# Recurrent part of a hybrid decoder layer: chunks of one 128-token tile instead of 64 tokens, groups of heads written out

## The chip, the core and the metric

The kernel runs on one core of one Trainium2 chip. The metric is the time of one execution on the device in microseconds, the median over several runs. The core has five engines that work side by side and meet at semaphores: PE (TensorE, matrix products, writes only to PSUM), DVE (VectorE), ACT (ScalarE), POOL (GpSimd) and SP, which here only issues DMAs. Each engine takes its instructions strictly in the order written.

## The reference, cut to what matters

One layer on x (256 tokens, 2048 wide), in float32: half a SwiGLU step, an input projection into an attention group and a recurrent group (RWKV-7), an output projection over both, half a SwiGLU step again, and a gated embedding. The change touches only the recurrent group, 16 heads of 64:

```
def step(state, inp):
    r_t, w_t, k_t, v_t, kk_t, a_t = inp
    sa = einsum('bhvk,bhk->bhv', state, -kk_t)
    state = (state * w_t[:, :, None, :]
             + sa[..., None] * (kk_t * a_t)[:, :, None, :]
             + v_t[..., None] * k_t[:, :, None, :])
    return state, einsum('bhvk,bhk->bhv', state, r_t)
...
decay = exp(-exp(w));  kk = kk / max(norm(kk), 1e-12);  k = k * (1 + (a - 1) * k_a)
o = (o - mean(o)) * rsqrt(var(o) + GN_EPS) * ln_x_w + ln_x_b
o = (o + sum(r * k * r_k) * v) * g
```

The recurrence over tokens isn't run token by token. Within a chunk of tokens it is a triangular system, which is inverted; from chunk to chunk a state of 64 x 64 per head is carried.

## The kernel before, in words

The order of the whole kernel is written out by hand, one program for each engine. Feed-forward, projections and the rest are products of three parts (`products`, L339 to L341) on weights that ACT and DVE split into a high and a low half (`split_hi` L316, `split_lo` L325). Between the input projection and the output projection lie attention (`pe_mla` and its counterparts) and then the recurrent part. It takes four heads at a time, a group, four groups in all (`GROUPS`). The 256 tokens are two tiles (`TT`) of 128. Each group has eight systems (`systems`): two tiles, two pairs of heads, two heads of a pair.

A group passes through these steps.

Loads and front. SP loads a group's r, k, v and the same rows one token earlier, with the parameters (`rwkv_loads`), once the group before has handed over v (`v_handed`) and made its inputs (`front_ready`). POOL mixes the two (`shift`, L915 and L923), and takes a square root (`power`, L662) for the unit keys. PE makes the gates in three parts (`pe_gates`, L1024 to L1037), with ACT behind each (`act_gates`), the last two giving cumulated decays within a chunk of 64 tokens. DVE does `front` in steps 1 to 5 (unit keys, mixed keys, the bonus) and `with_decay`, which multiplies four inputs by the decays.

Scores. PE turns the four inputs (`turn`, L1050), ACT and DVE copy them out (`act_alpha`, `act_scores`, `scores`), and PE multiplies all tokens of a tile with all (`pe_scores`, L1061 and L1067), 256 columns a product; DVE masks the result to the part of the triangle that lies within a chunk (L1353, tiles `AB` and `AK`).

Inverse. `pe_inverse` (L1079, L1089), `act_inverse` (L1237) and DVE's `inverse` (L1379, L1366) double the size of the inverted blocks level by level. `INV` has five levels, 2, 4, 8, 16, 32. A level is done in two halves `h` of four systems: PE makes q, ACT copies it to `Q`, PE makes x, DVE joins it to `XT` by a predicated copy and flips it to `X` by a transpose. The next level's q of a half waits for that half's join. Levels 0 and 1 (`EARLY`) of group r + 1 stand at the end of loop iteration r, levels 2 to 4 (`LATER`) at the start of the next. Between the `LATER` halves DVE does `front` of the following group, and PE its gates.

State. `pe_state`, `act_state` and DVE's `state` multiply the inverse by keys and values (L1105, L1110, L1115) and then go chunk by chunk, four chunks of 64 tokens: PE multiplies by the state (L1123, L1128), DVE makes U (L1405), PE adds the new state (L1135, L1136 and L1140, the last two on 64 rows), DVE scales it by a chunk's decay (L1411), ready in the tile `PCM` which POOL fills (`chunk_decay`, L930). ACT copies each chunk's output (L1267), and `add_inner` adds what comes from within the chunk (L1145, L1096).

Output. DVE centres the output by head (`out_centre`), POOL finishes it (`finish`: a scale, a power, the gate, the bonus, L915, L662 and L948), PE turns it (`pe_out`, L1163), ACT and DVE split it into the output projection's operands (`act_out`, `out_lo`). `pe_out` stands at the end of a loop iteration, so in PE's order between the `EARLY` levels of the next group and its `LATER` ones. ACT copies gate and bonus to their second tiles (`act_hand_over`) when `finish` has released them. POOL does `shift` of the next group after `finish` of the one before.

The groups run in a loop on each engine, with group 0's head and the last group's tail written out around it. After the last group PE goes on with the output projection (`w_out_block`).

## Time and profile before

| what | us |
|---|---|
| median of three runs (2259.79 to 2265.68) | 2260.6 |
| profiled execution | 2262.39 |
| its span | 2260.5 |
| PE busy in the span | 2147.1 (95%) |
| DVE busy | 1199.1 (53%) |
| ACT busy | 862.5 (38%) |
| POOL busy | 134.1 (6%) |
| groups of heads in the recurrent part | 4 |

The span is what the profile covers, from its first to its last instruction; the execution's time has the start and the end around it. Products of float32 data are two instructions each in the records (x16 stands for eight products), as are their weight loads. In a timeline row the columns are start, duration, engine, line, operation, result and inputs with their shapes, the count, and in brackets how long the engine had been idle and who released it. Rows of several instructions are merged, so their duration is from the first's start to the last's end, and the last one's end overlaps the start of what follows. The clock is PE's granted clock as a share of full speed.

### The profile page before, as it was taken

What the parts mean: (1) busy time and instruction counts of PE and PEld (TensorE: products, weight loads), DVE (VectorE), ACT (ScalarE), POOL (GpSimd) and SP (SyncE); (2) the same over time, 40 slices, a digit from 0 to 9 for tenths busy, and PEclk for the clock granted to TensorE, in tenths of its full rate; (3) what the DMA queues carried; (4) which work ended last, traced back from release to release, by engine and by line L of the source; (5) the groups of instructions that cost most, each with busy time, mean ns of one, the idle gap of its engine ahead of it and who ended that gap; (6) DMA issues with size and microseconds to landing.
All of it is one profiled execution on the core that took longest, in us unless ns stands there. A gap on an engine that the chain in (4) does not pass through costs nothing.

```text
span 2260.5 us, 25634 instructions
## 1 busy us (share of the span) xinstructions
PE 2147.1 (95%) x10216; PEld 1801.8 (80%) x10216; DVE 1199.1 (53%) x1062; ACT 862.5 (38%) x758; POOL 134.1 (6%) x83
## 2 busy tenths in 40 slices
PE   6999999999999999966988899999999999999998
PEld 5888888888887788755877788888888888888777
DVE  4455554555555544755656644555445555554644
ACT  5333333333333444523222233533333333333353
POOL 0000000000000000130334310000000000000000
PEclk9999999999999999987989999999999999999999
DMA  6555555555555476520111135555555555555444
GB/s 225 188 193 196 186 186 196 193 186 186 199 190 186 142 217 210 191 93 21 38 45 51 55 122 172 199 187 187 189 193 193 186 190 188 197 186 187 166 155 144
DMA packets 193519, 373.64 MB, mean 165 GB/s; under 512 B 6978, under 2 KB 22592, under 8 KB 193088
## 3 DMA queue, kind: packets, MB, share of 16 engines
q1 hardware_dynamic: 191888, 367.63, 49.0%
q0 software_dynamic: 1584, 5.35, 0.7%
q8 instruction: 33, 0.54, 0.1%
q14 instruction: 14, 0.11, 0.0%
HBM read 367.44 MB, written 5.52 MB: 165 GB/s over the span
## 4 chain that ended last, share of the span: by engine, by line
PE 54%; issue 36%; DVE 6%; POOL 2%; ACT 1%; DMA 1%; SPq 0%; POOLq 0%; DVEq 0%; ACTq 0%
PE PS L339 16%; PE PS L340 16%; PE PS L341 16%; DVE wlo L325 1%; POOL pv L915 1%; PE PS L1061 0%; PE PS L1089 0%; POOL zz L923 0%; PE PS L1136 0%; PE PS L389 0%; DVE sc L850 0%; PE PS L1145 0%; DMA x_resid<-in_x 0%; PE PS L354 0%; PE PS L1105 0%
## 5 line engine op out<-in xcount | busy, mean ns | idle before, releaser
L325 DVE TENSOR_TENSOR wlo<-raw,whi 128x2048 fp32r<-128x2048 f32 (+1 forms) x339 | 769.3, 2270 | 783.2 <-PE PS L341 774.3
L316 ACT ACTIVATE whi<-raw 128x2048 fp32r<-128x2048 f32 (+1 forms) x339 | 644.2, 1902 | 1035.4 <-PE PS L341 1023.6
L339 PE MATMUL PS<-whi,xT_hi 128*128 128x512 f32 (+2 forms) x1952 | 758.1, 388 | 11.0 <-DVE wlo L325 10.9
L341 PE MATMUL PS<-whi,xT_lo 128*128 128x512 f32 (+2 forms) x1952 | 754.7, 387 | 0.0
L340 PE MATMUL PS<-wlo,xT_hi 128*128 128x512 f32 (+2 forms) x1952 | 754.7, 387 | 0.0
L339 PEld LDWEIGHTS PS<-whi,xT_hi 128*128 128x128 f32 x1952 | 367.3, 188 | 86.4 <-DVE wlo L325 7.4
L341 PEld LDWEIGHTS PS<-whi,xT_lo 128*128 128x128 f32 x1952 | 367.1, 188 | 74.1
L340 PEld LDWEIGHTS PS<-wlo,xT_hi 128*128 128x128 f32 x1952 | 367.3, 188 | 72.6
L339 PE MATMUL PS<-whi,hT_hi 128*128 128x512 f32 x744 | 292.0, 392 | 6.9 <-DVE hT_lo L473 4.7
L340 PE MATMUL PS<-wlo,hT_hi 128*128 128x512 f32 x744 | 291.6, 392 | 0.0
L341 PE MATMUL PS<-whi,hT_lo 128*128 128x512 f32 x744 | 291.1, 391 | 0.0
L339 PEld LDWEIGHTS PS<-whi,hT_hi 128*128 128x128 f32 x744 | 140.8, 189 | 37.1 <-DVE hT_lo L473 5.2
L341 PEld LDWEIGHTS PS<-whi,hT_lo 128*128 128x128 f32 x744 | 141.0, 189 | 29.5
L340 PEld LDWEIGHTS PS<-wlo,hT_hi 128*128 128x128 f32 x744 | 140.8, 189 | 29.2
L482 DVE SCALAR_TENSOR_TENSOR x_resid<-PS,x_resid 128x512 f32<-128x512 f32 x184 | 118.1, 683 | 53.4 <-PE PS L341 53.4
L662 POOL TENSOR_TENSOR rstd<-rstd,con 128x2 f32<-128x2 f32 x6 | 6.2, 1042 | 1640.5 <-DVE rstd L657 1640.5
L1079 PE MATMUL PS<-XT,AB 128*128 128x128 f32 x320 | 47.4, 303 | 7.3 <-DVE XT L1379 7.0
L1079 PEld LDWEIGHTS PS<-XT,AB 128*128 128x128 f32 x320 | 43.1, 212 | 11.3 <-DVE XT L1379 8.7
L372 DVE SCALAR_TENSOR_TENSOR xT_lo<-PS,gains,xT_hi 128x256 fp32r<-128x256 f32 x64 | 26.6, 477 | 33.0 <-ACT xT_hi L363 32.9
L1237 ACT ACTIVATE Q<-PS 128x256 f32<-128x256 f32 x40 | 15.6, 389 | 72.9 <-PE PS L1079 72.9
L363 ACT ACTIVATE xT_hi<-PS,gains 128x256 fp32r<-128x256 f32 x64 | 25.2, 474 | 37.0 <-PE PS L354 37.0
L473 DVE TENSOR_TENSOR hT_lo<-PS,hT_hi 128x1024 fp32r<-128x1024 f32 x22 | 26.9, 1225 | 10.2 <-ACT hT_hi L435 10.0
(266 smaller groups left out, 1196.5 us busy)
## 6 DMA issues: line engine op xcount, KB each, us to landing
raw<-in_w_gate SPq DMA_DIRECT2D x88, 1024.0 KB, 5.0
raw<-in_w_up SPq DMA_DIRECT2D x88, 1024.0 KB, 5.0
raw<-in_w_down SPq DMA_DIRECT2D x88, 1024.0 KB, 5.0
raw<-in_w_in SPq DMA_DIRECT2D x28, 1024.0 KB, 5.4
raw<-in_w_out SPq DMA_DIRECT2D x16, 1024.0 KB, 5.0
raw<-in_w_ple_gate SPq DMA_DIRECT2D x16, 1024.0 KB, 5.1
z_scratch<-zst POOLq DMA_DIRECT2D x6, 512.0 KB, 6.2
raw<-in_w_q_b SPq DMA_DIRECT2D x3, 1024.0 KB, 5.2
```

What stands on the lines that cost most here:

```text
L316: nc.scalar.activation(whi[:, n % WHI, 0:wd], raw[:, n % RAW, 0:wd], ACT.Copy).then_inc(hi_ready, 1)
L325: nc.vector.tensor_tensor(wlo[:, n % WLO, 0:wd], raw[:, n % RAW, 0:wd], f32(whi[:, n % WHI, 0:wd]), ALU.subtract).then_inc(lo_ready, 1)
L339: nc.tensor.matmul(acc, a, whi[:, n % WHI, c], start=st, stop=False)
L340: nc.tensor.matmul(acc, a, wlo[:, n % WLO, c], start=False, stop=False)
L341: ins = nc.tensor.matmul(acc, b, whi[:, n % WHI, c], start=False, stop=en)
L363: ins = nc.scalar.activation(xT_hi[:, kt, :], PS[:, 2 + u % 2, j * SEQ:(j + 1) * SEQ], ACT.Copy, scale=gains[:, 16 * k + kt:16 * k + kt + 1])
L372: ins = nc.vector.scalar_tensor_tensor(xT_lo[:, kt, :], PS[:, 2 + u % 2, j * SEQ:(j + 1) * SEQ], gains[:, 16 * k + kt:16 * k + kt + 1], f3 ...
L473: nc.vector.tensor_tensor(hT_lo[:, :, :].rearrange("p (b j) s -> p b (j s)", b=2), PS[:, 6:8, :], f32(hT_hi[:, :, :]).rearrange("p (b j) s ...
L482: ins = nc.vector.scalar_tensor_tensor(x[:, t, j * COLS:(j + 1) * COLS], PS[:, b + t, :], factor, x[:, t, j * COLS:(j + 1) * COLS], ALU.mu ...
L915: g.tensor_tensor(o, a, b, op).then_inc(pool_chain, 1)
L1079: ins = nc.tensor.matmul(PS[:, HALF_BANKS[h][0], (s % 4) * P:(s % 4 + 1) * P], AB[:, s, 0:P], XT[:, s, :], start=True, stop=True)
L1237: nc.scalar.activation(even_cols(Q[:, 4 * h:4 * h + 4, :], l), even_cols(PS[:, HALF_BANKS[h][0], :].rearrange("p (s c) -> p s c", s=4), l) ...
```

## The change

The chunk becomes a whole tile of 128 tokens, so there are two chunks and only one update of the state, between the tiles. The decays are cumulated from the middle of a tile instead of from the start of a chunk (`cum_in`, `cum_ex`), and the state between the tiles is scaled by `between_tiles`, the product of two decays. `chunk_decay`, its tiles and the constant `two_heads` are gone. The masks cover a whole triangle. A score product becomes two, one for the first 64 tokens of a tile and one for the last 64, each 128 columns wide, the first on 64 columns of weights. The inverse gets a sixth level that joins the two halves of a tile, with products 64 columns wide. Products with values or U are 64 columns wide, one head each, where they were 128 (a pair) before. Y and the part of the output that comes from keys and values within a tile are made between the levels (`pe_value_parts`). The output is accumulated in one PSUM bank and copied once. The groups are written out instead of looped; every level and every fill has a place of its own: gates of the next group in levels 2 to 4, `out_centre` of the group before in three parts behind the half levels 1 to 3, `pe_out` and `out_lo` in level 3, `front` from the half level 5 on. POOL does `shift` of the next group first, then `finish` of the old one, `unit_keys` of the next, and `gate_norm`, which is `finish`'s first part put apart. `alpha`, `B_`, `gg` and `bonus` have two buffers, and the hand-over copies are gone.

```
-CHUNK = 64
+HC = P // 2
-        "cum_in": rate * (same & (s <= t)),
+        "cum_in": rate * ((s <= t) * 1.0 - (s < HC) * 1.0),
...
-        INV = LEVELS[1:]
-        EARLY, LATER = (0, 1), (2, 3, 4)
+        INV = LEVELS[1:] + (HC,)
+        GATES_AT = (2, 3, 4)
...
+        def score(s, bank, lhs, pr, t, par):
+            dst = PS[:, bank, (s % 2) * 256:(s % 2 + 1) * 256].rearrange("p (k c) -> p k c", k=2)
+            nc.tensor.matmul(dst[0:HC, :, 0:HC], lhs[:, par, pr, t * P:t * P + HC], ART[:, pr, t, :, 0:HC], start=True, stop=True)
+            return nc.tensor.matmul(dst[:, :, HC:P], lhs[:, par, pr, t * P:(t + 1) * P], ART[:, pr, t, :, HC:P], start=True, stop=True)
...
+        def pe_value_parts(pe, r, part):
+            if part == 0:
+                pe.wait_ge(ak_ready, 4 * r + 4)
+                pe.wait_ge(v_handed, r + 1)
+                for s, t, pr, par in systems():
+                    ins = nc.tensor.matmul(PS[:, 2, s * RN:(s + 1) * RN], AK[:, s, 0:P], vv[:, t, head(pr, par)],
+                                           start=s == 0, stop=s == 7)
+                ins.then_inc(y_done, 1)
+            elif part == 1:
+                for s, t, pr, par in systems():
+                    nc.tensor.matmul(PS[:, 3, s * RN:(s + 1) * RN], AK[:, s, P:256], vv[:, t, head(pr, par)], start=s == 0, stop=False)
+            else:
+                pe.wait_ge(heads_out, 2 + r)
+                for pr in range(2):
+                    cc = slice(pr * P, (pr + 1) * P)
+                    nc.tensor.matmul(PS[:, 2, cc], Kd[:, 0, cc], vv[:, 0, cc], start=pr == 0, stop=False)
...
 pe_inverse, behind the q products of a level:
+                if n in (1, 2, 4):
+                    pe_value_parts(pe, r, (1, 2, 4).index(n))
+                if n == 3 and r:
+                    pe_out(pe, r - 1)
+                if nxt is not None and n in GATES_AT:
+                    pe_gates(pe, nxt, n - GATES_AT[0])
...
 pe_state:
+            pe.wait_ge(up_ready, UP * r + UP)
+            pe.wait_ge(y_ready, r + 1)
+            for t in range(TT):
+                for s, _, pr, par in systems(4 * t, 4 * t + 4):
+                    ins = nc.tensor.matmul(PS[:, 6 + t, (s % 4) * RN:(s % 4 + 1) * RN], X[:, s, :], Y[:, s, :], start=s % 4 == 0, stop=s == 3)
+                ins.then_inc(w2_done, 1)
+                if t == 0:
+                    for s, _, pr, par in systems(4, 8):
+                        ins = nc.tensor.matmul(PS[:, 4, (s % 4) * P:(s % 4 + 1) * P], alpha[:, r % 2, 1, pr * P:(pr + 1) * P], X[:, s, :],
+                                               start=True, stop=True)
+                    ins.then_inc(w1_done, 1)
+            pe.wait_ge(u_ready, 2 * r + 1)
+            for pr in range(2):
+                cc = slice(pr * P, (pr + 1) * P)
+                ins = nc.tensor.matmul(PS[:, 2, cc], B_[:, r % 2, 0, cc], U[:, 0, cc], start=False, stop=pr == 1)
+            ins.then_inc(ds_done, 1)
+            own_tokens(pe, 0)
+            if nxt is not None:
+                turn(pe, nxt, 0)
+            pe.wait_ge(w1_ready, r + 1)
+            pe.wait_ge(s_ready, 2 * r + 2)
+            for pr in range(2):
+                ins = nc.tensor.matmul(PS[:, 7, pr * P:(pr + 1) * P], W1T[:, pr, :], S[:, pr, :], start=False, stop=pr == 1)
+            ins.then_inc(ws_done, 1)
+            for pr in range(2):
+                nc.tensor.matmul(PS[:, 3, 256 + pr * P:256 + (pr + 1) * P], ART[:, pr, 1, 1, :], S[:, pr, :], start=False, stop=False)
+            if nxt is not None:
+                turn(pe, nxt, 1)
+                turn(pe, nxt, 2)
+            pe.wait_ge(u_ready, 2 * r + 2)
+            own_tokens(pe, 1).then_inc(ou_done, 1)
+            if nxt is not None:
+                turn(pe, nxt, 3)
...
 DVE inverse, behind the join and flip of a half level:
+                        fill = 2 * n + h
+                        if r and fill in (1, 2, 3):
+                            out_centre(r - 1, fill - 1)
+                        if r and n == 3 and h == 1:
+                            out_lo(r - 1)
+                        if nxt is not None and fill >= 5:
+                            front(nxt, fill - 4)
+                        if nxt is None and n in (4, 5) and h == 1:
+                            split_lo(dve, WOUT + n - 4)
...
 DVE, a group:
+                scores(r)
+                inverse(r, nxt)
+                if nxt is not None:
+                    state_factor(nxt)
+                    for k in range(3):
+                        with_decay(nxt, k)
+                state(r, nxt)
...
 POOL:
+            shift(0)
+            unit_keys(0)
+            for r in range(GROUPS):
+                if r + 1 < GROUPS:
+                    shift(r + 1)
+                if r:
+                    finish(r - 1)
+                if r + 1 < GROUPS:
+                    unit_keys(r + 1)
+                gate_norm(r)
+            finish(GROUPS - 1)
```

## Rows read from the trace of the kernel before

**Rows 1.** The page, the span in 40 equal slices, PE's busy tenths

```profile
PE   6999999999999999966988899999999999999998
```

**Rows 2.** Timeline of PE, starts of the four groups and of the output products

```profile
1068.05 3.72 PE L1061 MATMUL PS<-ART,BTm 128*128 128x256 f32 x16 [0.44 <-ACT BTm L1219]
...
1128.03 3.72 PE L1061 MATMUL PS<-ART,BTm 128*128 128x256 f32 x16 [1.40 <-DVE ART L1344]
...
1196.14 3.72 PE L1061 MATMUL PS<-ART,BTm 128*128 128x256 f32 x16 [1.40 <-DVE ART L1344]
...
1260.77 3.50 PE L1061 MATMUL PS<-ART,BTm 128*128 128x256 f32 x15 [1.40 <-DVE ART L1344]
...
1315.06 0.48 PE L339 MATMUL PS<-whi,xT_hi 128*128 128x512 f32 x1
```

**Rows 3.** Timeline of PE between 1149 and 1208 us, cut

```profile
1149.17 1.12 PE L1163 MATMUL PS<-con,og 128*128 128x128 f32 x4 [5.79 <-POOL og L948]
...
1153.29 1.89 PE L1024 MATMUL PS<-wl,lora_t 65*128 65x256 f32 x8
...
1165.26 1.16 PE L1079 MATMUL PS<-XT,AB 128*128 128x128 f32 x8 [1.96 <-DVE XT L1379]
...
1172.62 2.39 PE L1105 MATMUL PS<-vv,AK 128*128 128x128 f32 x16
1174.85 1.95 PE L1110 MATMUL PS<-X,alpha 128*128 128x128 f32 x16
1176.64 1.95 PE L1115 MATMUL PS<-Y,X 128*128 128x128 f32 x16
...
1203.39 2.05 PE L1079 MATMUL PS<-XT,AB 128*128 128x128 f32 x16
...
1207.16 1.16 PE L1079 MATMUL PS<-XT,AB 128*128 128x128 f32 x8
```

**Rows 4.** Windows behind the 1.96 us: length, busy (count) by engine, clock, DMA

```profile
1166.00:1169.00 3.00, 3.00 (x16) 2.77 (x14) 1.91 (x3) 0.38 (x1) 0.00 (x0) 0.62 0.00 0
1169.00:1172.60 3.60, 3.60 (x17) 3.60 (x18) 1.40 (x4) 0.67 (x2) 0.00 (x0) 0.50 0.00 0
```

**Rows 5.** Timeline of PE, products of 2 columns, and of 64 beside 128 rows

```profile
1180.10 0.49 PE L1135 MATMUL PS<-S,con 128*128 128x128 f32 x2
1180.52 0.48 PE L1136 MATMUL PS<-vv,Kd 64*128 64x128 f32 x2
...
1234.56 0.50 PE L1037 MATMUL PS<-con,sigw 128*128 128x2 f32 x4
1234.92 0.68 PE L1035 MATMUL PS<-sigw,con 128*128 128x256 f32 x2
```

**Rows 6.** Timelines of DVE and ACT, operations beside POOL's shift, and ACT's copies

```profile
1156.12 0.43 DVE L1379 COPY_PREDICATED XT<-con,PS 128x256 f32<-128x256 uint32 x1 [4.22 <-issue]
...
1156.59 0.71 DVE L1366 STREAM_TRANSPOSE X<-XT 128x512 f32<-128x512 f32 x1
...
1159.59 0.69 DVE L1302 TENSOR_TENSOR kk<-zz,gc 128x512 f32<-128x512 f32 x1 [1.19 <-POOL zz L923]
...
1192.58 1.21 ACT L1219 ACTIVATE BTm<-PS 64x512 f32<-64x512 f32 x2
```

**Rows 7.** Timelines of DVE and POOL around 1000 us, in attention's second half

```profile
995.25 2.67 DVE L846 TENSOR_SCALAR mx<-mx 128x4 f32<-128x4 f32 x1
...
998.03 3.92 DVE L850 TENSOR_TENSOR sc<-sc,den 128x512 f32<-128x512 f32 x1
...
997.98 3.42 POOL L915 TENSOR_TENSOR pv<-pv,gc 128x1536 f32<-128x1536 f32 x1
```

**Rows 8.** Timelines of ACT and POOL, a group's loads from hand-over to landing

```profile
1068.02 0.63 ACT L1223 ACTIVATE vv<-zz 128x512 f32<-128x512 f32 x1
...
1080.95 3.44 POOL L915 TENSOR_TENSOR pv<-pv,zz 128x1536 f32<-128x1536 f32 x1 [16.77 <-DMA wl<-in_w_g]
```

**Rows 9.** Timeline of DVE ahead of the first group

```profile
1062.33 2.40 DVE L1335 TENSOR_TENSOR R__101<-pin,zz 128x512 f32<-128x512 f32 x1
```

More of the change, by code:

```diff
@@ L30 @@
 EPS, GN_EPS = 1e-6, 64e-5
-CHUNK = 64
-NCHUNK = SEQ // CHUNK
+HC = P // 2
 COLS = 512
@@ L1066, in pe_scores @@
             for s, t, pr, par in systems():
-                ins = nc.tensor.matmul(PS[:, s // 2, (s % 2) * 256:(s % 2 + 1) * 256], KTm[:, par, pr, t * P:(t + 1) * P],
-                                       ART[:, pr, t, :, :], start=True, stop=True)
+                if s == 6 and r:
+                    pe.wait_ge(o_copied, r)
+                ins = score(s, s // 2, KTm, pr, t, par)
                 if s % 2:
                     ins.then_inc(ak_done, 1)
-        def pe_inverse(pe, r, levels, nxt):
-            for n in levels:
-                last = n == len(INV) - 1
+        def pe_value_parts(pe, r, part):
[14 more added lines that the diff above has]
+                    nc.tensor.matmul(PS[:, 2, cc], Kd[:, 0, cc], vv[:, 0, cc], start=pr == 0, stop=False)
@@ L1366, in flip, with inverse @@
                 return v.transpose(dst[:, a:b, :].rearrange("p s c -> p (s c)"), src[:, a:b, :].rearrange("p s c -> p (s c)"))
-            def inverse(r, levels, nxt, before):
-                for n in levels:
-                    l, last = INV[n], n == len(INV) - 1
+            def inverse(r, nxt):
+                for n, l in enumerate(INV):
                     for h in range(2):
-                        dve.wait_ge(inv_x, 10 * r + 2 * n + h + 1)
-                        v.memset(gate_step[:, h:h + 1], 0.0)
+                        dve.wait_ge(inv_x, JOINED * r + 2 * n + h + 1)
@@ new lines, in state @@
+                dve.wait_ge(ds_done, r + 1)
+                for par in range(2):
+                    rows, c = slice(par * RN, (par + 1) * RN), slice(par * RN, (par + 1) * RN)
+                    v.tensor_tensor(S[rows, :, c], PS[rows, 2, 0:256].rearrange("p (a c) -> p a c", a=2)[:, :, c],
+                                    between_tiles[rows, r % 2, :].unsqueeze(2).broadcast_to([RN, 2, RN]), ALU.mult).then_inc(s_ready, 1)
+                if nxt is not None:
+                    with_decay(nxt, 3)
+                    turns(nxt)
```

433 lines of the change are left out of this document (162 added, 271 removed).

## The prediction

> **What bounds the kernel now.** First the page's slices: PE is busy to nine tenths nearly everywhere, and the one hole is slices 18 to 23 [rows 1]. Two stages lie there, attention and the recurrent part; the change touches the second. On PE's timeline it runs from the first `L1061` at 1068.05 us to the first output product at 1315.06, in four head groups that begin at 1068.05, 1128.03, 1196.14 and 1260.77 [rows 2], so 60.0, 68.1, 64.6 and 54.3 us, 247.0 in all. After it PE's queue is full, so that what this part gives back, the kernel gives back.
>
> Inside one group the reader is to see three things [rows 3]. (a) The inverse is bound by PE where nothing intervenes: a level begins 3.77 us after the one before (1203.39 to 1207.16), and eight 128-wide products take 1.79 (1174.85 to 1176.64), 0.224 each. (b) PE stands still at two places: 5.79 us until GpSimd has finished the group before, and 1.96 us until VectorE has joined a level; after the second the clock was 0.62, then 0.50, which is 1.2 GHz [rows 4]. (c) From the end of the inverse (1172.62) to the next group's scores (1196.14) pass 23.5 us, a chain of four 64-token chunks through PE, VectorE and ScalarE. This chain is what the change shortens.
>
> **What goes.** The chunk loop, `own_half` copies, the products of whole head pairs, GpSimd's `chunk_decay`, the two hand-over copies and the stop of PE for `pe_out` between two levels. `pe_out` now stands in level 3 of the next group, and GpSimd does the next group's `shift` ahead of the old group's `finish`.
>
> **What comes, on PE, per group.** A sixth level with 64 tokens on a side: 16 products of 64 columns. Two blocks of 8 such products between the levels (values), 8 for W2, 8 for the own tokens: 48 of 64 columns. Of these the trace has none. From below: the 2-column ones, two of them in 0.36 (1234.56 to 1234.92), 0.18 each. From above: where products of 64 and of 128 rows alternate, one takes 0.42 (1180.10 to 1180.52), say 0.41 [rows 5]. I take 0.20, between 0.18 and the 0.224 of 128 columns, because only the width of the moving side differs. The scores are 32 products of 128 columns instead of 16 of 256: at 0.224 that is 7.2, as much as now.
>
> The work of PE in a group without waits: 7.25 from the scores' start to level 0 (1196.14 to 1203.39, VectorE's masks and flip, unchanged), 3.75 for level 0, 4 x 3.6 (16 x 0.224) for levels 1 to 4, 3.2 for level 5, values 1.6 + 1.6 + 0.45, gates 1.73 + 1.73 + 1.66 (four 256-wide products show 1.89 busy, of which 0.16 lies over the next), `pe_out` 0.45. Then the state: W2 0.8, W1 0.9, W2 0.8, B x U 0.45, own tokens 0.8, turn 0.45, W1T x S 0.45, ART x S 0.45, two turns 0.9, and after the third turn ScalarE's two copies, 1.21 [rows 6], with 0.2 to reach it: 7.4, with the hop in front 7.5. S and its scaling (two VectorE operations of 128 columns on 64 rows, 0.6 for both, less than the 0.69 of one of 512) lie beside own tokens and turn. So 23.5 becomes 7.5, but levels and values pay 7 of the 16 back. In the last group there are no turns and the state is 6.0. Sums: 44.9 in group 0 (no `pe_out`), 45.3 in groups 1 and 2, 38.7 in group 3 (no gates).
>
> **The waits that remain.** VectorE walks a level in 2 x (0.43 + 0.71) [rows 6], under PE's 3.6, and between the levels it gets `front` and `out_centre`, operations of 0.69. Every such fill after a first half holds the second half's join. With its measured durations: 0.55 in level 1 (0.73-us joins), 1.3 in level 5 (`front` step 4, two of 0.69), 0.6 for the last copy, in every group with a successor.
>
> Larger is what GpSimd does to VectorE. VectorE's scaling of 4 columns (`mx`) began at 995.25 and took 2.67, until GpSimd went on to its next operation at 997.98. `sc`, of 512 columns, began 0.05 after that operation and took 3.92: GpSimd's 3.42 and then the 0.69 that 512 columns take alone, less what overlaps [rows 6, 7]. A join and a flip kept 0.43 and 0.71 while GpSimd's last shift operation ran, which ended ahead of 1159.59 [rows 6]. So a VectorE operation with two inputs in SBUF, and this scaling, wait for GpSimd's running operation. Where is that met? From the end of vv (1068.65) to GpSimd's start on the loaded group at 1080.95 pass 12.3 us [rows 8]; in the new order the three shift operations then run at 13.5 to 16.9, 17.0 to 20.4 and 20.5 to 24 after the scores' start, with no `finish` ahead of them. In just this stretch VectorE has `out_centre`: its scaling at 13.75 ends at 17.1; its subtraction at 18.2 waits for 20.45; its square, behind the third, ends at 25.2. The join of level 1's second half stands behind it and comes at 25.7, and PE, which gave the first half of level 2 at 17.55, has nothing until then. Waits of PE in groups 1 and 2: 0.55, 0.8 and 7.3 in levels 1 and 2; 2.65 in level 4 (`front` 2 and 3 against `gate_norm`, three operations that I put at 1.3: 3.42 x 512/1536 is 1.14), 0.45 for `heads_out`, 1.3 and 0.6 as above: 13.65, and 2 for the slow clock after the 7.3. So 45.3 + 13.65 + 2 = 61. `finish` of the old group (about 6, nearly all of the 5.79 that PE waits for it now) then ends at 31.4 and `pe_out` comes at 35, so that wait is gone; it is VectorE that is late next. Group 0 has no `out_centre`, only `gate_norm` against `front` (3.2): 44.9 + 0.55 + 3.2 + 1.3 + 0.6 + 1 for the clock = 51.5. Group 3 has no shift: 38.7 + 4.5 (0.55, 0.8, 1.9 against `finish`'s first, 0.55, 0.7) = 43.2.
>
> The Trainium skill's page SBUF — State Buffer, section "Who interferes with whom", says that a VectorE instruction with two SBUF inputs, or in a two-port mode as `tensor_scalar` can be, and a GpSimd instruction that reads SBUF lock each other out for a whole instruction, in the order of issue. The rows agree for the two operations above (2.67 and 3.92). By this rule the 7.3 stands; if the two merely shared the port, the sum would be rival B's.
>
> **Ahead of the first group** `R_` took 2.40 beside GpSimd's chunk decay, which goes [rows 9]: 1.7, of which 1.45 reach the scores. The other table and the one memset of the state lie ahead of that, in the shadow of PE's and ScalarE's gates: nothing, and less than 0.69, the time of twice its columns, without that cover. Behind the last group `finish` is as long as now, with two output blocks in front of its `pe_out`: nothing, and up to 5.79 without them.
>
> **Sum.** 51.5 + 61 + 61 + 43.2 = 216.7, less than 247.0 by 30.3; with the 1.45, 31.8 less. The profiled execution took 2262.4 us (span 2260.5, about 2 around it) and would take 2230.6; the median of the runs is 1.8 lower, so 2229.
>
> **Rivals.**
> B, GpSimd doesn't get in the way (its shift lands elsewhere in time, or the fills slip between): the same walk without locks gives 48.6, 55.5, 55.5 and 42.1, in which PE waits 2.95 for `finish` in level 3. 201.7, so 46.8 less: 2214. For it: contact depends on when the loads land, to a few us. Against: 10.4 of the first 24 us are GpSimd's, and the fills lie in them.
> C, the clock: every gap of 1.3 us or more is followed by a stretch at 1.2 GHz. After the 1.96 gap 3.0 us at 0.62 and 3.6 at 0.50 lost 1.1 and 1.8 [rows 4]. Nine such gaps (2, 3, 3, 1) at 2.9, of which 5 are counted: 21 more, 2250. For it: gaps in every level. Against: 1.40 before the scores isn't followed by one, levels 0 there step at 3.77.
> D, slower: the 48 narrow products and the 16 scores with 64-column weights don't hide their loads. At 0.41, 48 x 0.21 + 16 x 0.19 = 13.1 a group, 52 in all: 2281. It decides from 31.8 / (4 x 64) = 0.12 above my price, at 0.32 each. Against it: the 2-column ones at 0.18 and the eight of 0.224 each, whose weight loads must already overlap the products at full width.
> The skill's page TensorE: Matmul & The Clock Gate, section "The mechanism", says that a weight load overlaps a running product only if it goes to another row group. By that a narrow product would take two loads and its stream, over 0.4, and D would hold. The trace disagrees: all 128 rows are in use in the 0.224.
> E, no change: unrolled groups wait for instructions, or fill and stall eat the rest. The code before this part is straight too and PE doesn't stop in it (nines in slices 15 and 16) [rows 1].
>
> **Numbers.** Forecast 0.55 (own range 2218 to 2240), B 0.20, C 0.13, D 0.05, E 0.04, and 0.03 beyond. A measurement of this kernel can tell 0.3%, 7 us, from no change. Slower by more 0.05, within 0.04, faster 0.91. The range, 2205 to 2252, takes in B and most of C.
>
> **What would show it.** Distance of the first `score` products of two groups: about 51, 61, 61, and 43 to the first output product. From level 5's last product to the next scores 8 us. Level 1's second `out_centre` operations beside GpSimd's shift 2 to 4 us long instead of 0.69, and PE idle 5 to 8 us in level 2 of groups 1 and 2 but not of 0 and 3. 64-wide products every 0.18 to 0.22. Wrong, if the narrow ones take over 0.3, if PE idles longer behind `pe_out` than in level 2, or if the group ends at 55 without long VectorE operations.

## The result: slower by 0.8%, where 1.4% faster was forecast

| | before | after |
|---|---|---|
| median | 2262.35 us (4 runs) | 2281.64 us (4 runs, 2275.19 to 2282.92) |
| ratio, 95% interval | | 1.0079 [1.0054, 1.0103] |
| profiled execution, span | 2262.39, 2260.5 | 2282.92, 2281.1 |
| groups 0 to 3 | 60.0, 68.1, 64.6, 54.3 = 247.0 | 71.4, 71.8, 75.2, 48.9 = 267.3 |
| forecast for the groups | | 51.5, 61, 61, 43.2 = 216.7 |

The forecast was 2229 (2205 to 2252), with 0.05 for slower. Of the 20.6 us by which the profiled span grew, 20.3 lie in the part that the prediction was about, the four groups; it begins 0.6 us earlier and what follows it is 0.9 longer.

### The profile page after: what moved, and what is told of

It is laid out like the page before. It is cut to its first block, busy times and chain, and to the rows that moved or that the text cites. A ratio compares the mean times of both kernels' runs of the same rounds, so it can differ in the third digit from the quotient of the medians.

```text
span 2281.1 us, 25192 instructions
## 1 busy us (share of the span) xinstructions
PE 2175.5 (95%) x10232; PEld 1815.6 (80%) x10232; DVE 1194.0 (52%) x1043; ACT 855.8 (38%) x726; POOL 120.6 (5%) x79
## 4 chain that ended last, share of the span: by engine, by line
PE 56%; issue 36%; DVE 7%; ACT 1%; DMA 1%; SPq 0%; POOL 0%; ACTq 0%; DVEq 0%
PE PS L331 16%; PE PS L332 16%; PE PS L333 16%; PE PS L1056 1%; PE PS L1055 1%; DVE wlo L317 1%; DVE X L1364 1%; DVE XT L1374 1%; PE PS L1134 1%; PE PS L381 0%; DVE sc L842 0%; DMA x_resid<-in_x 0%; PE PS L1048 0%; PE PS L1099 0%; PE PS L346 0%
## 5 line engine op out<-in xcount | busy, mean ns | idle before, releaser
L1099 PE MATMUL PS<-XT,AB 128*128 128x128 f32 (+1 forms) x384 | 56.4, 299 | 19.1 <-DVE XT L1374 15.7
L1099 PEld LDWEIGHTS PS<-XT,AB 128*128 128x128 f32 x384 | 51.2, 210 | 22.5 <-DVE XT L1374 17.6
L1374 DVE COPY_PREDICATED XT<-con,PS 128x256 f32<-128x256 uint32 x32 | 16.2, 505 | 48.0 <-issue 46.5
L355 ACT ACTIVATE xT_hi<-PS,gains 128x256 fp32r<-128x256 f32 x64 | 25.2, 474 | 37.0 <-PE PS L346 37.0
```

Of the source, the lines that this page charges most:

```text
L355: ins = nc.scalar.activation(xT_hi[:, kt, :], PS[:, 2 + u % 2, j * SEQ:(j + 1) * SEQ], ACT.Copy, scale=gains[:, 16 * k + kt:16 * k + kt + 1])
L1099: ins = nc.tensor.matmul(PS[:, HALF_BANKS[h][0], (s % 4) * P:(s % 4) * P + w], AB[:, s, 0:P], XT[:, s, 0:w], start=True, stop=True)
L1374: v.copy_predicated(even_cols(XT[:, mine, :], l), joins(l, 1, 4), even_cols(src, l)).then_inc(low_ready, 1)
```

## The profile after

PE (TensorE) is busier than before (2175.5 us against 2147.1) and the kernel slower. The page's rows of PE and of its granted clock (40 slices, tenths) show why that can be:

```profile
PE   6999999999999999967989899999999999999998
PEclk9999999999999999976888899999999999999999
```

Slices 19 and 22 are fuller than they were [rows 1], and the clock is below nine over six slices, 18 to 23. The windows of the four groups and of the whole part say how much (columns as in [rows 4]: length, busy and count of PE, PEld, DVE, ACT, POOL, then granted clock, DMA share, GB/s):

```profile
1067.47:1138.87 71.40, 66.87 (x389) 56.23 (x389) 34.61 (x68) 15.17 (x30) 16.06 (x7) 0.75 0.13 38
1138.87:1210.63 71.76, 64.17 (x393) 56.81 (x393) 42.65 (x75) 16.26 (x32) 21.79 (x11) 0.81 0.13 41
1210.63:1285.88 75.25, 67.94 (x392) 60.53 (x392) 41.03 (x75) 16.35 (x32) 21.48 (x11) 0.77 0.13 39
1285.88:1334.78 48.90, 45.54 (x349) 39.51 (x349) 30.87 (x58) 12.25 (x21) 9.50 (x7) 1.00 0.21 69
1067.47:1334.78 267.31, 244.52 (x1521) 213.07 (x1521) 149.16 (x276) 60.03 (x112) 68.83 (x36) 0.82 0.15 45
```

The same part of the kernel before, whole:

```profile
1068.05:1315.06 247.01, 216.89 (x1504) 199.94 (x1505) 151.91 (x295) 67.61 (x146) 79.75 (x39) 0.93 0.17 48
```

Length times clock estimates what a group would last at full speed: 53.6, 58.1, 57.9 and 48.9, in all 218.5 after; before, with clocks of 0.94, 0.90, 0.95 and 0.94 in its four groups, 230.1. By this estimate the change did shorten the work, by 11.6 us, and lost 48.8 us to the low clock where the kernel before lost 16.9. The forecast had 211.7 and 5. The estimate also shrinks waits for other engines, which PE's clock doesn't shorten, so it comes out somewhat low; the runs below with PE kept busy measure the same parts at 224.3 (after_all_warm) and 238.7 (before_kept_warm), extra products included.

PE's timeline, the starts of the groups (answering to [rows 2] and [rows 3]):

```profile
1067.47 0.69 PE L1055 MATMUL PS<-ART,BTm 128*64 128x128 f32 x2 [0.44 <-ACT BTm L1222]
1068.09 0.80 PE L1056 MATMUL PS<-ART,BTm 128*128 128x128 f32 x2
...
1138.87 0.43 PE L1055 MATMUL PS<-ART,BTm 128*64 128x128 f32 x2
1139.23 0.49 PE L1056 MATMUL PS<-ART,BTm 128*128 128x128 f32 x2
1139.65 0.43 PE L1055 MATMUL PS<-ART,BTm 128*64 128x128 f32 x2
...
1151.27 1.95 PE L1099 MATMUL PS<-XT,AB 128*128 128x128 f32 x16
```

A score's two products take 0.36 and 0.42 from start to start, 0.78 for both, where two of 0.224 were put down. Level 0 begins 12.40 us after the first score (1151.27 - 1138.87) instead of 7.25, and in group 0, where all is at 1.2 GHz, 21.4. Further on in group 1:

```profile
1157.35 1.90 PE L1080 MATMUL PS<-vv,AK 128*128 128x64 f32 x16
...
1165.62 2.07 PE L1099 MATMUL PS<-XT,AB 128*128 128x128 f32 x8 [3.58 <-DVE XT L1374]
1167.49 3.52 PE L1085 MATMUL PS<-vv,AK 128*128 128x64 f32 x16
1170.80 3.73 PE L1014 MATMUL PS<-wl,lora_t 65*128 65x256 f32 x8
1174.32 3.62 PE L1118 MATMUL PS<-Q,X 128*128 128x128 f32 x16
...
1186.57 1.16 PE L1099 MATMUL PS<-XT,AB 128*128 128x128 f32 x8 [2.00 <-DVE XT L1374]
```

The same eight narrow value products take 1.74 at full clock (1157.35 to 1159.09) and 3.31 behind the gap; the 12 us from 1165.6 to 1177.6 are all at 0.50, without a pause. The gap itself comes from the lock that the prediction named: operations of DVE (VectorE) wait for a running one of POOL (GpSimd), here in group 1:

```profile
1157.65 2.70 DVE L1419 TENSOR_SCALAR hsg<-hsg 128x8 f32<-128x8 f32 x1
...
1161.50 2.88 DVE L1421 TENSOR_TENSOR oo<-oo,hsg 128x512 f32<-128x512 f32 x1
```

```profile
1156.88 3.44 POOL L907 TENSOR_TENSOR pv<-pv,gc 128x1536 f32<-128x1536 f32 x1
1160.39 3.43 POOL L915 TENSOR_TENSOR zz<-zz,pv 128x1536 f32<-128x1536 f32 x1
```

## The experiments

All times are medians in us; the ratio is to the kernel before on the same chip. "Part" is the four groups of one profiled execution, and the clocks are those of its groups. That execution can lie at an end of its kernel's spread: for scores_whole (2264.46), scores_in_pairs (2275.78, of 2246.85 to 2275.78), scores_whole_centre_first (2252.34) and after_kept_warm (2257.44) it is the slowest, for centre_first_kept_warm (2216.63), all_gaps_warm (2210.49) and after_all_warm (2229.41) the fastest. Outside the part the profiled executions spend 2003.6 to 2020.3 us. So a difference of a few us between two medians doesn't rank two kernels.

| run | median | ratio, interval | part | clock of the groups |
|---|---|---|---|---|
| scores_whole | 2256.88 | 0.9979 [0.9969, 0.9990] | 250.2 | 0.93 0.75 0.75 0.96 |
| scores_wide_weights | 2257.69 | 0.9980 [0.9966, 0.9995] | 246.7 | 0.87 0.76 0.76 0.96 |
| scores_in_pairs | 2262.78 | 1.0005 [0.9980, 1.0030] | 258.0 | 0.85 0.77 0.77 1.00 |
| before_split_scores | 2292.05 | 1.0144 [1.0103, 1.0185] | 277.6 | 1.00 0.95 0.83 0.80 |
| scores_whole_kept_warm | 2231.67 | 0.9875 [0.9844, 0.9905] | 214.8 | 1.00 1.00 1.00 0.96 |
| scores_whole_short_shift | 2222.02 | 0.9824 [0.9796, 0.9853] | 214.5 | 0.97 0.84 0.91 1.00 |
| scores_whole_centre_first | 2239.06 | 0.9891 [0.9856, 0.9926] | 233.0 | 0.91 0.79 0.81 0.93 |
| before_kept_warm | 2255.14 | 0.9973 [0.9960, 0.9985] | 238.7 | 0.98 1.00 1.00 1.00 |
| after_kept_warm | 2253.24 | 0.9947 [0.9927, 0.9968] | 240.3 | 0.81 1.00 1.00 0.90 |
| centre_first_kept_warm | 2226.75 | 0.9857 [0.9831, 0.9884] | 209.8 | 0.99 1.00 1.00 0.96 |
| all_gaps_warm | 2220.81 | 0.9827 [0.9808, 0.9846] | 206.9 | 1.00 1.00 1.00 1.00 |
| after_all_warm | 2239.69 | 0.9918 [0.9895, 0.9942] | 224.3 | 1.00 1.00 1.00 1.00 |
| x_first_level2 | 2245.24 | 0.9944 [0.9921, 0.9968] | 227.5 | 0.93 0.87 0.87 1.00 |
| x_first_levels24 | 2231.01 | 0.9873 [0.9826, 0.9920] | 216.3 | 0.97 0.89 0.89 1.00 |
| centre_and_x_first | 2223.80 | 0.9833 [0.9811, 0.9856] | 209.4 | 0.99 0.91 0.97 0.93 |
| all_warm_x_first | 2215.36 | 0.9808 [0.9781, 0.9834] | 203.2 | 1.00 1.00 1.00 1.00 |

### What do the split scores cost?

scores_whole puts back one product of 256 columns per score:

```
-nc.tensor.matmul(dst[0:HC, :, 0:HC], lhs[:, par, pr, t * P:t * P + HC], ART[:, pr, t, :, 0:HC], ...)
-return nc.tensor.matmul(dst[:, :, HC:P], lhs[:, par, pr, t * P:(t + 1) * P], ART[:, pr, t, :, HC:P], ...)
+return nc.tensor.matmul(dst, lhs[:, par, pr, t * P:(t + 1) * P], ART[:, pr, t, :, :], ...)
```

> The changed kernel with its score products whole again, one of 256 columns on 128 columns of weights per system, all else as changed. Theory W (weights of 64 and of 128 columns in turn cost more than either, and such a stretch doesn't bring the clock back): from the first score product to level 0 7.2 us instead of 12.4, in each of four groups, so 20.6 less, and the clock comes up inside group 0's scores, 10 us or more less there: 2245 to 2258 us. Rival L (the gaps that GpSimd's locks tear into PE's queue are what costs, through the clock): the stretch may be 7.2, but shift then meets more of out_centre, gaps of 5 to 8 us in level 2 instead of 3.6 and 2.4, and 2270 us or more.

scores_wide_weights keeps 32 products of 128 columns and gives all of them 128 columns of weights:

```
-nc.tensor.matmul(dst[0:HC, :, 0:HC], lhs[:, par, pr, t * P:t * P + HC], ART[:, pr, t, :, 0:HC], ...)
+nc.tensor.matmul(dst[:, :, 0:HC], lhs[:, par, pr, t * P:(t + 1) * P], ART[:, pr, t, :, 0:HC], ...)
```

> The changed kernel with its 32 score products of 128 columns, but all of them on 128 columns of weights (the first of each pair fills the lower half too, which the mask sets to zero). If the width of the weights in turn is what costs: 0.224 us a product, 7.2 us to level 0, as with whole products, 2245 to 2258 us. If the short or the strided moving side costs: 0.36 to 0.42 a product as changed, 12.4 us, and about 2280.

scores_in_pairs keeps the changed kernel's products and their sizes, and orders them 64, 64, 128, 128 by the columns of their weights:

```
+for k in range(2):
+    nc.tensor.matmul(dst[0:HC, :, 0:HC], lhs[:, pk, pr, t * P:t * P + HC], ART[:, pr, t, :, 0:HC], ...)
+for k in range(2):
+    ins = nc.tensor.matmul(dst[:, :, HC:P], lhs[:, pk, pr, t * P:(t + 1) * P], ART[:, pr, t, :, HC:P], ...)
```

> The changed kernel with two products on 64 columns of weights and then two on 128, so half as many switches of width, same products. If each switch costs (0.17 us more than 0.224): 9.8 us to level 0 instead of 12.4, 10 us less in all and more with the clock: 2262 to 2272. If each narrow load costs whatever its neighbour: 12.4 and about 2280.

From the first score to level 0 at full clock pass 12.40 us in the changed kernel, 7.24 in scores_whole, 7.37 in scores_wide_weights, 9.68 in scores_in_pairs. PE's timeline, wide weights first, then pairs:

```profile
1119.09 0.39 PE L1055 MATMUL PS<-ART,BTm 128*128 128x128 f32 x2
1119.32 0.39 PE L1056 MATMUL PS<-ART,BTm 128*128 128x128 f32 x2
```

```profile
1128.83 0.65 PE L1058 MATMUL PS<-ART,BTm 128*64 128x128 f32 x4
1129.41 0.71 PE L1062 MATMUL PS<-ART,BTm 128*128 128x128 f32 x4
```

So 32 products of 128 columns do cost the 0.224 each that the forecast had (7.37 in all, 0.23 each). What costs is the change between 64 and 128 columns of weights: 32 changes take 5.2 us, 16 take 2.4, 0.15 to 0.16 each, with the same number of narrow weight loads in both. The rows from before had such a price already: where 64 and 128 rows alternate, a product takes 0.42 [rows 5]. The Trainium skill's page TensorEngine Tiling (Array Packing), section Tiling Modes, Key Properties, says that a change of the tiling mode, "not just tile", drains the engine. The rows agree in that a change of shape costs time, 0.16 us; that these plain products count as two tiling modes, and that the time is a drain, no run here shows. Products of one narrow shape in a row don't pay it: eight of level 5, all with 64 columns of weights, take 0.15 each (below).

before_split_scores gives the kernel before the split scores, and nothing else:

```
-ins = nc.tensor.matmul(PS[:, 4 + s // 2, ...], BTm[:, par, pr, t * P:(t + 1) * P], ART[:, pr, t, :, :], ...)
+ins = score(s, 4 + s // 2, BTm, pr, t, par)
```

> The kernel before with only its score products split as in the change (the first 64 tokens of a tile on 64 columns of weights, the last 64 on 128). Theory W: 12.4 us instead of 7.3 to level 0 in four groups, 20.6 more, and up to 10 more where the clock was low when the scores began: 2280 to 2295. Rival L: no more than the 5 us a group that the pitch gives, or nothing if the pitch comes from the new banks or order: 2260 to 2265.

It loses 30.2 us, more than 4 x 5.2: the scores take 12.4, 12.4, 19.95 and 19.89. In group 2 the clock falls inside them, 2 us after a wait of 1.40, while PE is busy all the time:

```profile
1198.20:1200.00 1.80, 1.80 (x10) 1.14 (x10) 1.36 (x3) 0.27 (x1) 0.73 (x1) 1.00 0.51 142
1200.00:1202.00 2.00, 2.00 (x8) 1.23 (x6) 0.54 (x1) 0.00 (x0) 0.00 (x0) 0.55 0.73 192
```

The same wait in the kernel before [rows 2] isn't followed by a low clock, and neither is it in group 1 here (12.4), so the fall doesn't come each time. But whole scores alone bring 24.8 of the 52.6 us between the result and the forecast. By length times clock the groups of scores_whole are worth 50.7, 56.5, 56.3 and 43.6 at full speed, where 50.5, 59, 59 and 43.2 were forecast; they last 54.5, 75.3, 75.0 and 45.4. What is missing is clock. It is low behind the gap in level 2, which two operations of VectorE held by GpSimd make (PE's row, then VectorE's):

```profile
1146.11 2.08 PE L1098 MATMUL PS<-XT,AB 128*128 128x128 f32 x8 [7.54 <-DVE XT L1373]
```

```profile
1138.03 3.74 DVE L1420 TENSOR_TENSOR oo<-oo,hsg 128x512 f32<-128x512 f32 x1
1141.80 3.79 DVE L1289 TENSOR_TENSOR tmp<-oo 128x512 f32<-128x512 f32 x1
```

### Is it the gaps?

scores_whole_kept_warm fills PE's gaps with products whose result nobody reads:

```
+if h == 1:
+    for _ in range({2: 7 if r else 0, 4: 2, 5: 1}.get(n, 0) if nxt is not None else 0):
+        nc.tensor.matmul(PS[:, HALF_BANKS[1][0], :], ident, con[:, 0:COLS], start=True, stop=True)
```

> The changed kernel with one 256-column product per score again, and PE kept busy in its gaps: ahead of the second half's q products of a level it runs extra products of 128x512 (their result is overwritten, nothing is computed from it), 7 in level 2, 2 in level 4 and 1 in level 5, in groups 1 and 2 (in group 0 the 2 and the 1). At 0.9 us each they last about as long as the gaps (7.54, 2.83, 1.15). Theory (the gaps cost twice: themselves, and the slow clock that follows each): without any idle time the granted clock of groups 1 and 2 comes near 1.0 and each lasts about 57 to 60 us instead of 75.3 and 75.0, group 0 about 52; the kernel about 2222 to 2235. Rival 1 (the narrow products and the 65-row gates pull the clock down or keep it down whatever precedes them): clock 0.75 to 0.8 stays, groups 72 to 78, kernel 2255 to 2262. Rival 2 (the extra products are themselves too long and delay the levels): clock near 1.0 but groups of 63 to 66.

```profile
1068.97:1120.17 51.20, 49.22 (x363) 44.36 (x363) 34.38 (x68) 15.18 (x30) 16.07 (x7) 1.00 0.18 52
1120.17:1179.23 59.06, 56.35 (x380) 47.45 (x380) 46.06 (x75) 16.26 (x32) 22.03 (x11) 1.00 0.17 50
1179.23:1238.40 59.17, 56.35 (x381) 47.45 (x381) 46.17 (x75) 16.27 (x32) 22.03 (x11) 1.00 0.17 50
1238.40:1283.75 45.35, 42.04 (x317) 39.38 (x317) 30.55 (x58) 12.25 (x21) 9.49 (x7) 0.96 0.22 76
```

More work, and 25.2 us less (23.5 by the ratios). With whole scores and filled gaps the groups come near the forecast's (51.2, 59.1, 59.2, 45.3 for 51.5, 61, 61, 43.2), and the median near 2229. On its timeline the narrow products can be read without the low clock, 0.15 for 64 columns of weights and 0.216 for 128:

```profile
1146.51 1.90 PE L1084 MATMUL PS<-vv,AK 128*128 128x64 f32 x16
1148.24 1.95 PE L1014 MATMUL PS<-wl,lora_t 65*128 65x256 f32 x8
...
1169.76 1.22 PE L1120 MATMUL PS<-X,Q 128*64 128x64 f32 x16
```

The next two go at the origin of the largest gap. scores_whole_short_shift leaves out most of the token mixing, so that GpSimd's three operations are short:

```
-tt(pv3[:, :, :, :], pv3[:, :, :, :], zz[:, :, :, :], ALU.subtract)
+tt(pv3[:, 0:1, 0:1, 0:64], pv3[:, 0:1, 0:1, 0:64], zz[:, 0:1, 0:1, 0:64], ALU.subtract)
```

> The changed kernel with one 256-column product per score, and GpSimd's mixing of a group's rows with the ones before cut to 64 columns of one tile (most of the token mixing is left out of the computation; loads and order stay). Theory (VectorE's out_centre waits for GpSimd's 3.4 us operations by a lock, and that is the 7.54 us gap in level 2): the subtraction and the square there take 0.7 instead of 3.74 and 3.79, the gap in level 2 goes to below 1.5 us, and with it the low clock that follows it; groups 1 and 2 about 62 to 66 instead of 75, kernel 2236 to 2245. Rival (out_centre comes too late for another reason, its copy or its place in the order): the gap stays at 5 or more, kernel 2255.

VectorE's two operations fall from 3.74 and 3.79 in scores_whole to what they cost alone, and the gap in level 2 from 7.54 to 1.35:

```profile
1132.99 0.65 DVE L1420 TENSOR_TENSOR oo<-oo,hsg 128x512 f32<-128x512 f32 x1
1133.68 0.69 DVE L1289 TENSOR_TENSOR tmp<-oo 128x512 f32<-128x512 f32 x1
```

It gave 35 us, where 12 to 21 were expected. Groups 1 and 2 are 32.1 us shorter in the profiles, for gaps that shrank by 12.9 us in levels 2 and 4 together: the price of a gap is more than twice the gap. scores_whole_centre_first keeps the shift and moves VectorE's work ahead of it:

```
-if r and fill in (1, 2, 3): out_centre(r - 1, fill - 1)
+if r and fill == 0: out_centre(r - 1, 0); out_centre(r - 1, 1)
+if r and fill == 3: out_centre(r - 1, 2)
```

> The changed kernel with one 256-column product per score, and VectorE's first two parts of out_centre moved from behind the half levels 1 and 2 to behind the first half of level 0, ahead of GpSimd's shift; the third part stays in level 1. Theory (the lock): reduce, scaling, subtraction and square take 0.69 each there, done by 12 us after the scores' start, before GpSimd's operations begin at about 13.5; the gap of 7.54 in level 2 falls to 2 or less, and 1 to 2 us of waiting come in level 1 instead. Groups 1 and 2 about 64 to 70 instead of 75; kernel 2238 to 2250. Rival 1 (the lock only moves to the square or the third part): a gap of 3 to 4 stays, 2250 to 2256. Rival 2 (the gap costs nothing, since what follows it waits for GpSimd's finish anyway): 2255.

The lock is gone (subtraction and square 0.69 each) and the gap 2.59, in level 1; 17.8 us less by the medians, and 20.1 less in groups 1 and 2. The clock, 0.79 and 0.81, is still low behind the gaps that stay.

before_kept_warm fills the gaps of the kernel before:

```
+keep_warm(6)   # ahead of pe_out
+keep_warm(2)   # ahead of the last level's second q
```

> The kernel before, with extra products of 128x512 on PE in its own two idle places: 6 ahead of pe_out, where it waits 5.8 us for GpSimd, and 2 ahead of the last level's second q, where it waits 1.96 us (nothing is computed from them). Theory (a gap is followed by a slow clock in this kernel too, and that costs what the clock 0.93 of these 247 us says): clock of the four groups 0.98 to 1.0, the part 235 us or less instead of 247, kernel 2248 to 2252. Rival (the low clock in it belongs to the chain of short products behind the inverse, not to the gaps): clock stays 0.93, kernel 2260 to 2264.

The clock rose as expected; the part fell only to 238.7, not to 235 or less, and the kernel by 7, not by 10 to 14. So the kernel before has little to get there, and the changed one much.

### The changed kernel itself, kept warm

after_kept_warm has the split scores and 3, 2 and 1 extra products in levels 2, 4 and 5; after_all_warm has 5 more ahead of group 0:

```
+for part in range(3):
+    keep_warm((0, 1, 3)[part]); pe_gates(pe, 0, part)
+keep_warm(1)
```

> The changed kernel itself, with its split scores, and only PE's gaps filled with extra products of 128x512 ahead of the second half's q: 3 in level 2 (groups 1 and 2), 2 in level 4, 1 in level 5. Theory (two terms: the split scores cost 5.2 us a group by their pitch, and all the rest of the loss is the slow clock behind the gaps): groups 1 and 2 have clock 0.95 to 1.0 and take about 60 us (their full-speed 58) instead of 71.8 and 75.2; scores to level 0 stays 12.4; the kernel about 2245 to 2258, so 12 to 20 more than the kept-warm kernel with whole scores (2231.67). Rival (the mixed-width scores lower the clock by themselves): clock under 0.9 in groups 1 and 2 also with the gaps filled, or a stretch of 0.50 that begins within the scores; kernel 2265 or more. Group 0's scores at 1.2 GHz (21.4 us) are open: if what precedes them set them, they stay at 18 to 21.

> The kernel after_kept_warm, with the same extra products ahead of the first group (1, 3 and 1). Theory (the split scores don't lower the clock, but a clock that is low when they begin stays low until they end): the first scores begin at full clock and take 12.4 us instead of 21.4, group 0 falls from 66.9 to about 57, the kernel to 2242 to 2247. Rival (the low clock of group 0 has nothing to do with the idle time ahead of it): 21.4 stays, kernel 2253.

```profile
1056.48:1112.78 56.30, 54.36 (x395) 46.10 (x395) 34.34 (x68) 15.17 (x30) 16.10 (x7) 1.00 0.16 48
1112.78:1172.70 59.92, 57.78 (x404) 47.59 (x404) 41.62 (x75) 16.24 (x32) 21.82 (x11) 1.00 0.17 49
1172.70:1232.42 59.72, 57.77 (x404) 47.59 (x405) 41.21 (x75) 16.25 (x32) 21.81 (x11) 1.00 0.18 49
1232.42:1280.79 48.37, 45.53 (x348) 39.50 (x349) 30.40 (x58) 12.23 (x21) 9.50 (x7) 1.00 0.21 68
```

This is the changed kernel with 20 extra products and without the slow clock: 42 us faster by the medians, 36 by the ratios. In the profile of after_kept_warm the scores of group 0 still took 21.4; with the idle places ahead of them filled they take 12.4. Low when they begin, the clock stays low until they end. But it doesn't always begin low where the places are left idle. In before_split_scores the granted clock was 0.53 in the 4 us ahead of the first score, 0.50 in the changed kernel, and the same split scores ran at 1.00. And the nine executions of after_kept_warm form two clusters, 2242.55 to 2245.05 and 2253.24 to 2257.44, with the profiled one in the slower. Group 0's 9 us would make such a difference, though no profile of the faster cluster shows it; so the 13.6 us between the medians of these two kernels are partly chance. In groups 1 and 2 the split costs only 0.9 and 0.6 us against the whole scores kept warm: its 5.2 us lie over part of the lock's gap (3.58 against 7.54).

### Why is a gap dearer here than before?

Before, the 5.79 us gap [rows 3] was followed by 4 us at the low clock, from 1149.17 to 1153.2. The windows from 1.1 us behind its end:

```profile
1150.30:1153.20 2.90, 2.90 (x16) 2.90 (x16) 0.69 (x1) 0.98 (x2) 2.82 (x2) 0.52 0.02 5
1153.20:1157.60 4.40, 4.40 (x35) 4.19 (x33) 1.45 (x5) 2.75 (x4) 4.32 (x2) 1.00 0.22 56
```

Behind it stood pe_out and eight q products of full size, 128 columns on 128x128 weights. In scores_whole four q products stand behind the gap of level 2, then the narrow and the 65-row products:

```profile
1146.11:1148.00 1.89, 1.89 (x9) 1.89 (x10) 1.43 (x3) 0.00 (x0) 0.89 (x2) 0.50 0.00 0
1148.00:1151.30 3.30, 3.30 (x18) 3.30 (x17) 0.00 (x0) 1.67 (x2) 3.14 (x3) 0.50 0.00 0
1151.30:1154.80 3.50, 3.50 (x9) 2.79 (x10) 0.00 (x0) 0.00 (x0) 0.52 (x1) 0.50 0.24 74
1154.80:1158.20 3.40, 3.40 (x17) 3.39 (x16) 1.14 (x3) 1.08 (x2) 0.00 (x0) 0.50 0.00 1
```

x_first_level2 leaves the gap and puts four more full products behind it; x_first_levels24 does so in level 4 too:

```
+if n == 2:        # n in (2, 4) in the second
+    x_products(0)
 if n in (1, 2, 4): pe_value_parts(...)
 ...
+for h in range(1 if n == 2 else 0, 2): x_products(h)
```

> The kernel scores_whole with one change in PE's order of level 2: the four x products of the first half stand directly behind the second half's q, ahead of the narrow value products and the 65-row gate products; the 7.5 us gap ahead of that q stays. Theory (the kind of work behind a gap decides when the clock comes back): eight full products of 128x128x128 now follow the gap without a break, as behind the 5.79 us gap of the kernel before; the clock is 1.0 again 4 us after the gap, the value products take 1.9 instead of 3.5, the gates 1.9 instead of 3.7; 4 to 5 us less in each of groups 1 and 2, kernel 2246 to 2250 instead of 2256.88. Rival (the low clock lasts a time set by the gap, whatever runs): 12 us at 0.50 stay, kernel 2254 to 2259.

> The kernel x_first_level2 with the same order in level 4 too, behind the 2.8 us gap: four x products of the first half ahead of the token state's products, the third gate part and its 2-column products. Theory: full clock again 4 us behind that gap in groups 0, 1 and 2 instead of 8.7, 1.5 to 2.5 us less a group at most, 4 to 7 in all below x_first_level2. Rival (low clock of fixed length): the same time as x_first_level2. Against both: the gates come 0.9 us later for ScalarE, which may delay the third copy.

```profile
1145.41:1147.28 1.87, 1.87 (x9) 1.87 (x9) 1.43 (x3) 0.00 (x0) 0.86 (x2) 0.50 0.00 0
1147.28:1149.00 1.72, 1.72 (x10) 1.72 (x10) 0.00 (x0) 1.46 (x2) 1.64 (x2) 0.52 0.00 0
1149.00:1152.50 3.50, 3.50 (x26) 3.29 (x26) 1.14 (x3) 0.21 (x1) 2.05 (x2) 1.00 0.03 10
```

With a gap of 6.69 still there, the clock is back 3.6 us behind it, about as before the change, and the kernel is 11.6 us faster than scores_whole (8 by the ratios), with the same products. Group 2 shows the same, with the same 6.69. The second gave 14.2 more where 4 to 7 were expected, but its four executions spread from 2220.64 to 2238.57. In the profiles the part fell by 11.2, and length times clock with it, from 207.0 to 201.2, so more than the clock is at work; that the half's join and flip come earlier too would explain it, and isn't shown here by itself.

### Putting it together

centre_first_kept_warm (2 extra products in level 1, 2 in 4, 1 in 5), all_gaps_warm (also ahead of group 0 and in group 3), centre_and_x_first (no extra products) and all_warm_x_first combine the edits above.

> Whole scores, out_centre's first two parts behind the first half of level 0, and PE's gaps filled with extra products of 128x512: 2 ahead of the second q of level 1 (groups 1 and 2), 2 in level 4, 1 in level 5. Theory (locks and clock are the two separate losses): the gap of level 2 is gone and needs no filling, clock 0.97 to 1.0, groups about 51, 53, 53, 45, in all 202 to 206; the kernel about 2219 to 2226, and so better than each remedy alone (2231.67 and 2239.06). Rival (the two remedies save the same time): 2230.

> The kernel centre_first_kept_warm, with more of PE's idle places filled: ahead of the first group 1 product of 128x512 before the second gate part, 3 before the third and 1 before the turns (idle 1.18, 3.08 and 1.64 us there, granted clock 0.50 from 1060 to the first scores), and in group 3 2 in level 1 and 1 in level 5. Theory (idle time is all that lowers the clock): the clock at the first scores is 1.0, group 0 loses nothing at its start, group 3 goes from 46.4 to about 44.5; the kernel 1 to 4 below the 2226.75 of the one without. Rival (the products there run at 1.2 GHz themselves, 1.7 us each, and delay the gates): 1 to 5 above it.

> Whole scores, out_centre's first two parts behind the first half of level 0, and in levels 2 and 4 the first half's x products directly behind the second half's q. No extra products. Theory (two separate savings: centre first took 17.2 us off the part of 250.2, x first 33.9): they share the level 2 gap, so less than their sum; groups about 51, 59, 59, 43, in all 210 to 216, kernel 2222 to 2230. Rival (the x order needs full products behind every gap; the 2.6 us gap now lies in level 1, where the order is as before, and narrow products follow it): 222 or more, 2234 to 2240.

> The kernel all_gaps_warm (2220.81) with the x order of levels 2 and 4. Theory (that order works through the clock alone): the same, 204 to 208 for the part, 2218 to 2223. Rival (the earlier x products also bring VectorE's joins forward): 2 to 4 us less in the part, 2214 to 2218.

The first fell just short (2226.75 for 2219 to 2226, part 209.8 for 202 to 206): with VectorE early, PE waits 1.46 us for GpSimd's og in level 3, rival B's wait:

```profile
1140.96 0.66 PE L1177 MATMUL PS<-con,og 128*128 128x128 f32 x4 [1.46 <-POOL og L940]
```

The second gave 5.9 us in the medians instead of 1 to 4, with overlapping intervals; its part is 2.9 shorter. The third came out as expected in the median, with the part at 209.4, just below the 210 to 216. In the last the rival held: at a clock of 1.00 throughout, the x order still takes 3.7 us off the part. centre_and_x_first is 1.7% faster than the kernel before without a wasted product, and 2.4% faster than the change (0.9833 / 1.0079). all_warm_x_first has the lowest median, 1.9% [1.7, 2.2] below before; its interval overlaps with those of all_gaps_warm and centre_and_x_first.

## Why the prediction was wrong

The part was to last 216.7 and lasted 267.3, 50.6 more. By length times clock that is 6.8 at full speed (218.5 against 211.7) and 43.8 of clock (48.8 against 5). By after_all_warm, which lasts 224.3 without the low clock, it is at most 12.6 and at least 38.0. Either way the clock is the larger share by far.

The step that failed first is "the scores are 32 products of 128 columns instead of 16 of 256: at 0.224 that is 7.2, as much as now". They are 12.4, so 5.2 us a group more. The prediction priced the narrow products "because only the width of the moving side differs", and that was right (0.216 for its 0.20); in the scores the weights' side differs, and there the 0.42 of [rows 5], used only as an upper bound for the others, was the price. Rival D had the scores in it, for half of them (3.0 us a group), and held the narrow products for the larger part; that its 2281 is the measured time is luck, by another sum. The rule set beside it, that of the Trainium skill's page TensorE: Matmul & The Clock Gate, section "The mechanism", on overlapping loads, was rightly held against the trace's 0.224; the one on the change of the tiling mode was not weighed.

The larger step that failed is the clock, put at 1 + 2 + 2 us where some 43 to 49 were lost. The prediction counted a low clock once in each of the first three groups, priced by what stands behind the 1.96 us in the kernel before [rows 4]; rival C took 2.9 for each of nine gaps (21 more, 2250). But in those rows the work behind a gap is the old one. The change puts narrow products and 65-row gates directly behind the first half of a level, and split scores behind the idle places ahead of group 0, and in both places the clock stayed at 1.2 GHz: 12 us behind a gap of 3.58, 21.4 us in group 0. x_first_level2 (on whole scores) and after_all_warm show it by taking the one or the other away. C had the right mechanism and, with 26.1 for all gaps, a little over half of the loss; it had no term for a low clock through group 0's scores.

Right were: the lock and its place. Its size was not: PE waits 3.58 and 2.43 in level 2 of groups 1 and 2, below the 5 to 8 that the prediction named. In scores_whole, whose scores have the length that was forecast, it is 7.54 (6.68 in group 2) for 7.3. The way there differs: VectorE's scaling began just ahead of GpSimd's first operation and took 0.17, where it was to wait 3.35. But the square, behind GpSimd's third, still ended 25.1 us after the scores' start, for 25.2. Right were also, in scores_whole, the gap in level 4 (2.83 for 2.65) and in level 5 (1.15 for 1.3), that PE doesn't wait for pe_out, and the state at full clock, 8.2 us from level 5's last product to the next scores in scores_whole_kept_warm for 8 (10.3 to 13.3 in the changed kernel, in part at 1.2 GHz). The part began 0.6 earlier, where 1.45 was put. That the shorter chain of chunks saves time is borne out by 2231.67 with whole scores and filled gaps.

Open: whether the narrow products or the 65-row ones, each alone, keep the clock low; they were only moved together. That a low clock follows idle time is shown by filling it; from what length on is not. What sets the level at which group 0's scores begin is open too, since it differs between executions with the same work ahead: scores_whole and scores_whole_kept_warm run the same program up to there, and their first eight scores took 4.28 and 3.72.

## What to carry to other kernels

Before splitting a matrix product, look at the shapes of the weights that will then follow each other: here each change between 64 and 128 columns cost 0.16 us, and a whole product of 128 columns 0.224. Where the split has to stay, order the products by shape, so that fewer changes are left. A gap on PE is priced by what runs behind it, so let full-size products come first there, and read a change's clock anew instead of taking it from rows in which other work follows. And where PE is at fault only through its clock, a kernel can get faster by doing more: fill the gap first, as a test of what it is worth, and then look for the order that closes it.

## What the runs showed of the hardware

- A change between 64 and 128 columns of weights costs 0.16 us at full clock (scores_wide_weights, scores_in_pairs); at 1.2 GHz the two products take 0.62 and 0.72 instead of 0.36 and 0.42.
- The granted clock can fall to 1.2 GHz while PE is busy without a pause, in a stretch of such changes (0.55 from 1200 us on in before_split_scores), and stays there for 21.4 us of them. The same stretch keeps 1.00 in all four groups of after_all_warm, where 0.69 us of idle time or none stand directly ahead of it.
- Behind a gap of 6.69 us, full products of 128x128x128 bring 2.4 GHz back in 3.6 us (x_first_level2); behind 7.54 us, with narrow and 65-row ones after the first four, PE was busy for 12 us at 0.50 (scores_whole).
- VectorE's scaling of 8 columns took 2.70 beside GpSimd's operation, 0.17 otherwise (scores_whole). The Trainium skill's page SBUF — State Buffer, section Who interferes with whom, has this as an exclusive lock for a whole instruction; the rows shown here agree (2.70, 2.88, 3.74 and 3.79 beside GpSimd's operations).
